# Splitting GpSimd's low-part subtraction of the input projection units into four instructions of 256 columns

## The chip, the cores and the metric

The kernel runs on one core of a Trainium2 chip. The metric is the device time of one execution, in microseconds (us). Each time is the median of several executions; the time before is 1633.45 us (three runs, 1633.38 to 1634.8).

## What is computed

One inference step of a two-layer streaming encoder, for 512 prompt tokens and 32 sample tokens (544 columns), model width 1024. Each layer, cut to what matters:

```
hn = rmsnorm(x, norm_mix)
parts = split_columns(hn @ w_in)          # w_in: 1024 x 2856, all four head groups
o_a = gated_delta(conv(q, k, v), ...)     # causal conv width 4, then chunk-wise delta rule
o_b = sink_attention(rope(s_q), ...)      # sliding window
o_c = mla_attention(...)                  # latent attention
o_d = c_b * causal_dwconv(c_c * c_x)
x = x + concat([o_a, o_b, o_c, o_d]) @ w_out
x = x + square(relu(rmsnorm(x) @ mlp_w1)) @ mlp_w2
x = x + (pl @ ple_w_proj) * sigmoid(rmsnorm(x) @ ple_w_gate)
```

## The kernel before

Activations lie with features on the 128 partitions and tokens along the columns. Weights come in *units* of 128 x 1024 (one output tile of 128 features against all 1024 input features, 512 KB). Every matmul by weights is done in three passes, for precision: each weight is split into a high part in a reduced format (`w_high`) and the rest (`w_rest`), each activation likewise, and the product adds high x high, high x rest and rest x high. A unit therefore passes four steps:

1. SyncE starts the DMA into one of two `raw` buffers (`load_unit`), once the unit that used the buffer has its low part made (`lo_done`).
2. ScalarE writes the high part (`high`, line 869) and raises `hi_done`. It first waits for the product of the unit two before, whose place in `w_high` it takes.
3. GpSimd writes the low part, raw minus high (`rest`, line 763), and raises `lo_done`.
4. TensorE multiplies (`product`, line 1702; `first_units`, line 1722, for the first two units of a layer; `unit_part`, line 1757, in quarters between attention tasks), after waiting for `lo_done`.

Units 0 to 22 of a layer are the input projection, 23 to 30 (`U_OUT`) the output projection, then come the MLP and the gate. All orders are written out by hand: every engine runs its own program in order, and semaphores tie them.

Around the change, in each layer: the first two units are multiplied tile by tile as VectorE makes the low part of `hidden` (line 1214) and, in the first layer, sums the squares (lines 1589 and 1590). Units 1 to 6 are q, k and v of the delta rule. For each, VectorE multiplies the product by the rms (line 1231), runs a convolution of four instructions (line 1247, then line 1250 three times, each waiting for the one before) and copies two tails of three columns (lines 1297 and 1298), after which ScalarE applies silu (line 1078). L2 norms of q and k follow (ScalarE lines 949 to 960, VectorE line 1571), and the first `prep` step on TensorE (line 1803) waits for all four. Units 7 to 14 are multiplied in halves with steps of the delta rule between them. Units 15 to 22 are spread over the attention: for each task TensorE makes scores, VectorE takes the minimum (line 1441), ScalarE the exponential, VectorE scales the probabilities (lines 1449 and 1450), TensorE turns them (line 1893) and multiplies by the values (line 1913). `rest` of unit u+2 is made when the product of unit u is done.

Of the kernel before, what the change touches and what calls it, by code (L numbers as in the profile page):

```python
# [18 lines left out]
F32 = mybir.dt.float32  # L19
F32R = mybir.dt.float32r  # L20
ALU = mybir.AluOpType
# [5 lines left out]
D = 1024  # L27
# [27 lines left out]
U_OUT = N_IN  # L55
# [59 lines left out]
def weight_no(u):  # L115

    return output_of(u) if u < U_PLE else O_PLE + u - U_PLE

def place_of(u):  # L120

    if u < U_MLP:
        return 2 * (u % 2)
    if u < U_PLE:
        g, i = divmod(u - U_MLP, 2 * KT)
        return (2 + 2 * KT * g + 7 * PAIRS * g + 2 * i) % RING
    return 2 * ((u - U_PLE) % 2)
# [61 lines left out]
def raw_place(l, u):  # L189

    a = 1 - l
    if u < U_MLP:
        return (u + l) % 2
    if u < U_PLE:
        return (a, 2, 3, 1 - a)[(u - U_MLP) % 4]
    return (a, 1 - a)[(u - U_PLE) % 2]
# [132 lines left out]
def build(nc, w_units, w_kv, params, consts, x_t, p_t, conv_state, ckv_cache, kpe_cache, k_cache, v_cache,  # L329
          s_state, sconv_state, y_t, gdn_s_p, gdn_s_s, conv_p, conv_s, swa_k_p, swa_k_s, swa_v_p, swa_v_s,  # L330
          ckv_p, ckv_s, kpe_p, kpe_s, sconv_p, sconv_s):
    with ExitStack() as ctx:
# [120 lines left out]
        def signal(name, per, head=0):  # L453
            every.append(Signal(ctx.enter_context(nc.semaphore(name)), per, head))
            return every[-1]
# [13 lines left out]
        lo_done = signal("lo_done", O_PLE + 2 + KT, 4)  # L469
# [118 lines left out]
        def in_ring(base, more, s, n):  # L588

            return (base if s < 4 else more[s // 2 - 2])[:, (s if s < 4 else s % 2) * 512:][:, 0:n * 512]  # L590

        def whi_at(l, s, n):
            return in_ring(whi, [w[l] if isinstance(w, list) else w for w in whi_more], s, n)

        def wlo_at(l, s, n):
            return in_ring(wlo, wlo_more, s, n)
# [4 lines left out]
        def raw_at(l, u):  # L601
            s = raw_place(l, u)
            return raw[:, s, :] if s < 2 else raw_more[:, s - 2, :]
# [39 lines left out]
        def mark(ins, sig):  # L643

            ins.then_inc(sig.sem, 1)
            sig.made += 1
# [103 lines left out]
        def _(pool):  # L750
# [8 lines left out]
            def rest(l, u):  # L759

                pool.wait_ge(*hi_done.at(l, weight_no(u) + 1))
                s = place_of(u)
                mark(pool.tensor_tensor(wlo_at(l, s, 2), raw_at(l, u), whi_at(l, s, 2).bitcast(F32), ALU.subtract), lo_done)  # L763

            def pair_rest(l, g, p, k):

# [10 lines left out]
            def rest_of(l, work):  # L777

                for w in work:
                    if len(w) == 1:  # L780
                        rest(l, *w)
                    else:
                        pair_rest(l, *w)
# [39 lines left out]
            for l in range(DEPTH):  # L823

                wait_apart(pool, normed.at(l, 0))
                mark(pool.memset(qkv[:, :, TOK:TOKP], 0.0), pad_done)
                for u in range(SPLIT):
                    rest(l, u)
                add_square(l, 0, KT - 1)
                for u in range(N_PRE):  # L830
                    mid_unit(l, 2 * u)
                    rest(l, u + SPLIT)
                    mid_unit(l, 2 * u + 1)
                for u in range(N_PRE, N_IN):
                    rest(l, u + SPLIT)
                for m in range(KT):
                    rest(l, U_OUT + SPLIT + m)
                    add_square(l, 1, m)
                for i in (2, 3):
                    rest(l, U_MLP + i)  # L840
                rest_of(l, due(0, -2, 2))
                for g in range(GROUPS):
                    rest_of(l, due(g, 0, 2 * KT))
                    for p in range(PAIRS):
                        rest_of(l, due(g, 2 * KT + 7 * p, 7))
                        if g == GROUPS - 1:
                            add_square(l, 2, 2 * p)
                            add_square(l, 2, 2 * p + 1)
                for m, u in enumerate(range(U_PLE + SPLIT, UNITS)):
                    rest(l, u)  # L850
                    if m:
                        add_square(l, 3, m - 1)
# [1358 lines left out]
```

## Time and profile before

| | |
|---|---|
| median of 3 runs | 1633.45 us (1633.38 to 1634.8) |
| the profiled execution | 1635.42 us, of which the span from first to last instruction 1633.6 us |
| TensorE busy | 1533.8 us (94%) |
| VectorE busy | 1042.8 us (64%) |
| GpSimd busy | 834.8 us (51%), 473 instructions |
| GpSimd line 763 | 146 instructions of 1024 columns, 46 of them for input projection units |
| granted TensorE clock | 0.981 on average |

PE is TensorE's matmul, PEld its weight load, DVE VectorE, ACT ScalarE, POOL GpSimd. Times in rows are in us from the start of the span, unless marked ns. An engine's busy time includes time in which a started instruction is held up, so a row that is longer than its like is an instruction that waited inside.

### The profile page before, as it was taken

Reading aid. Unit: us, or ns where it says so; the run is one execution under the profiler, and the core shown is the slowest. Engines: PE = TensorE matmul, PEld = TensorE weight load, DVE = VectorE, ACT = ScalarE, POOL = GpSimd, SP = SyncE. Lnnn points to the kernel's source line nnn. Section 1 sums busy time; section 2 is a strip of 40 time slices with the busy share of each in tenths; the row PEclk is TensorE's granted clock in tenths of the full one; section 3 lists DMA queues with packets and bytes.
Section 4 is the critical chain, followed back from the end, with each engine's and each line's share of the span. In section 5 each row is a group of like instructions: output and inputs, shape, how many; then the busy total and the mean of one; then the engine's idle time right before and its main releaser. Section 6 shows DMA issues by size and latency. Waiting matters only on the chain.

```text
span 1633.6 us, 33883 instructions
## 1 busy us (share of the span) xinstructions
PE 1533.8 (94%) x14198; PEld 1445.6 (88%) x14198; DVE 1042.8 (64%) x1754; ACT 669.9 (41%) x1186; POOL 834.8 (51%) x473
## 2 busy tenths in 40 slices
PE   6999998899999999998899999988999999999895
PEld 6889786699999999988898997767999999999795
DVE  6865567456848566595577645754478594756953
ACT  6521233444544343453345213334354444434432
POOL 3344121065766849486533531202668576684952
PEclk9999999899999999999999999998999999999998
DMA  5211011133241414213222110102332324141121
GB/s 196 77 41 41 27 40 40 33 118 104 69 139 52 130 53 123 77 48 106 83 79 65 41 41 27 40 27 60 116 92 89 104 75 134 52 130 52 54 90 68
DMA packets 43960, 123.81 MB, mean 76 GB/s; under 512 B 10976, under 2 KB 13792, under 8 KB 43552
## 3 DMA queue, kind: packets, MB, share of 16 engines
q1 hardware_dynamic: 43664, 119.86, 23.8%
q8 instruction: 113, 1.85, 0.5%
q10 hardware_dynamic: 144, 1.78, 0.3%
q14 instruction: 39, 0.32, 0.1%
HBM read 117.86 MB, written 3.76 MB: 74 GB/s over the span
## 4 chain that ended last, share of the span: by engine, by line
PE 74%; DVE 13%; POOL 6%; ACT 4%; issue 3%; DMA 0%; POOLq 0%; DVEq 0%; SPq 0%; ACTq 0%
PE psum_p L1702 39%; PE psum_t L1743 15%; PE psum_p L1757 6%; PE psum_t L1772 5%; POOL w_rest L775 3%; DVE conv_out L1250 2%; PE psum_p L1913 1%; POOL x_squares_summed L794 1%; PE psum_p L1722 1%; PE psum_p L1893 1%; DVE probs L1450 1%; PE psum_p L1765 1%; POOL w_rest L763 1%; PE psum_t L1883 1%; PE psum_t L1886 1%
## 5 line engine op out<-in xcount | busy, mean ns | idle before, releaser
L1702 PE MATMUL psum_p<-hidden,w_high 128*128 128x272 f32 x3904 | 661.8, 292 | 13.8 <-POOL w_rest L763 6.2
L1702 PEld LDWEIGHTS psum_p<-hidden,w_high 128*128 128x128 f32 x3904 | 557.8, 190 | 19.7 <-POOL w_rest L763 7.2
L763 POOL TENSOR_TENSOR w_rest<-raw,w_high 128x1024 fp32r<-128x1024 f32 x114 | 278.3, 2445 | 469.5 <-ACT w_high L869 469.5
L1702 PE MATMUL psum_p<-hidden,w_rest 128*128 128x272 f32 x1952 | 405.5, 289 | 0.0
L1702 PEld LDWEIGHTS psum_p<-hidden,w_rest 128*128 128x128 f32 x1952 | 308.1, 190 | 0.0
L775 POOL TENSOR_TENSOR w_rest<-w_sums,w_high 128x512 fp32r<-128x512 f32 x128 | 206.0, 1634 | 93.3 <-DVE w_sums L1493 55.3
L869 ACT ACTIVATE w_high<-raw 128x1024 fp32r<-128x1024 f32 x114 | 120.2, 1056 | 239.7 <-PE psum_p L1702 168.1
L1743 PE MATMUL psum_t<-hidden_split_a,w_high 128*128 128x272 f32 x896 | 178.6, 290 | 13.1 <-issue 7.7
L1743 PE MATMUL psum_t<-hidden_split_b,w_high 128*128 128x272 f32 x896 | 177.0, 288 | 0.4 <-DVE hidden_split_b L1509 0.4
L1743 PEld LDWEIGHTS psum_t<-hidden_split_a,w_high 128*128 128x128 f32 x896 | 140.0, 188 | 17.6 <-issue 16.1
L1743 PEld LDWEIGHTS psum_t<-hidden_split_b,w_high 128*128 128x128 f32 x896 | 140.3, 188 | 0.8 <-DVE hidden_split_b L1509 0.8
L1743 PE MATMUL psum_t<-hidden_split_b,w_rest 128*128 128x272 f32 x448 | 129.0, 288 | 0.0
L1743 PE MATMUL psum_t<-hidden_split_a,w_rest 128*128 128x272 f32 x448 | 128.8, 288 | 0.0
L883 ACT ACTIVATE w_high<-w_sums 128x512 fp32r<-128x512 f32 x128 | 79.7, 628 | 117.0 <-DVE w_sums L1491 61.5
L1517 DVE SCALAR_TENSOR_TENSOR rope_in<-psum_p,rms 128x544 f32<-128x544 f32 x64 | 46.2, 722 | 114.7 <-PE psum_p L1702 102.7
L763 POOL TENSOR_TENSOR w_rest<-raw_more,w_high 128x1024 fp32r<-128x1024 f32 x32 | 80.4, 2522 | 54.0 <-ACT w_high L869 54.0
L794 POOL TENSOR_TENSOR x_squares_summed<-x_squares_summed,x_squared 128x544 f32<-128x544 f32 x43 | 69.8, 1623 | 57.7 <-ACT x_squared L938 49.8
L1214 DVE SCALAR_TENSOR_TENSOR hidden<-x,parameters,hidden 128x544 fp32r<-128x544 f32 x48 | 77.5, 1615 | 30.4 <-ACT hidden L932 29.7
L908 ACT ACTIVATE hidden_parts<-rope_in 128x544 f32<-128x544 f32 x64 | 42.2, 659 | 128.4 <-DVE rope_in L1517 128.4
L1757 PE MATMUL psum_p<-hidden,w_high 128*128 128x272 f32 x512 | 91.7, 301 | 0.0
L775 POOL TENSOR_TENSOR w_rest<-raw,w_high 128x512 fp32r<-128x512 f32 x48 | 76.0, 1590 | 29.0 <-ACT w_high L883 29.0
L1743 PEld LDWEIGHTS psum_t<-hidden_split_a,w_rest 128*128 128x128 f32 x448 | 84.3, 188 | 0.0
(284 smaller groups left out, 2534.8 us busy)
## 6 DMA issues: line engine op xcount, KB each, us to landing
raw<-w_units SPq DMA_DIRECT2D x146, 512.0 KB, 3.6
raw_more<-w_units SPq DMA_DIRECT2D x64, 512.0 KB, 3.6
x<-x_t SPq DMA_DIRECT2D x8, 272.0 KB, 6.0
y_t<-y SPq DMA_DIRECT2D x8, 272.0 KB, 2.1
constants<-consts ACTq DMA_DIRECT2D x1, 1737.5 KB, 7.8
ple_in<-p_t SPq DMA_DIRECT2D x2, 544.0 KB, 4.5
constants<-consts SPq DMA_DIRECT2D x1, 1088.0 KB, 5.8
w_kv<-w_kv SPq DMA_DIRECT2D x2, 256.0 KB, 5.2
```

The source lines that it names most:

```text
L763: mark(pool.tensor_tensor(wlo_at(l, s, 2), raw_at(l, u), whi_at(l, s, 2).bitcast(F32), ALU.subtract), lo_done)
L775: mark(pool.tensor_tensor(wlo_at(l, s, 1), src, whi_at(l, s, 1).bitcast(F32), ALU.subtract), lo_done)
L794: ins = pool.tensor_tensor(sumx[:], sumx[:], sqx[:, m % 2, :], ALU.add)
L869: mark(act.activation(whi_at(l, place_of(u), 2), raw_at(l, u), ACT.Copy), hi_done)
L883: mark(act.activation(whi_at(l, s, 1), src, ACT.Copy), hi_done)
L908: link(act, act.activation(dst, two(xr[:]), ACT.Square), h_sq, l)
L1214: mark(dve.scalar_tensor_tensor(ha[l][:, m, 1, :], x[:, m, :], g, f(ha[l][:, m, 0, :]), ALU.mult, ALU.subtract), normed)
L1517: link(dve, dve.scalar_tensor_tensor(two(xr[:]), psum_of(l, o), 0.0, two(rms[:]), ALU.max, ALU.mult), freed, l)
L1702: ins = pe.matmul(pp[:, 2 * b + h, 0:HALF], w(l, s, 2)[:, cols(k)], rhs[:, k, part, h * HALF:(h + 1) * HALF], start=(n == 0 and z == 0), s ...
L1743: ins = pe.matmul(bank, w(l, s, 1)[:, j * P:(j + 1) * P], hs(l, j)[:, half, part, :], start=(j == 0 and z == 0), stop=(j == PAIRS - 1 and ...
L1757: ins = pe.matmul(pp[:, h, 0:HALF], w(l, s, 2)[:, k * P:(k + 1) * P], ha[l][:, k, half, h * HALF:(h + 1) * HALF], start=(k == 0 and z == 0 ...
L1772: ins = pe.matmul(dst[r, j * C:(j + 1) * C], lhsT(r), rhs(r), start=True, stop=True)
```

## The change

For units below `U_OUT`, `rest` issues four subtractions of 256 columns in place of one of 1024. The operands, the place in the order and both semaphores stay: the wait on `hi_done` stands before the first of the four, and `lo_done` is raised by the last. Other units keep the one instruction.

```diff
             def rest(l, u):
 
                 pool.wait_ge(*hi_done.at(l, weight_no(u) + 1))
-                s = place_of(u)
-                mark(pool.tensor_tensor(wlo_at(l, s, 2), raw_at(l, u), whi_at(l, s, 2).bitcast(F32), ALU.subtract), lo_done)
+                s, n = place_of(u), D // 4 if u < U_OUT else D
+                for a in range(0, D, n):
+                    ins = pool.tensor_tensor(wlo_at(l, s, 2)[:, a:a + n], raw_at(l, u)[:, a:a + n],
+                                             whi_at(l, s, 2).bitcast(F32)[:, a:a + n], ALU.subtract)
+                mark(ins, lo_done)
```

The order of GpSimd's instructions at the start of the first layer, before (`x_squares_summed` is the sum of squares, `hi_done` the signal of the high part):

```order
L763 TENSOR_TENSOR w_rest<-raw,w_high 128x1024 [waits hi_done] x2
L794 TENSOR_TENSOR x_squares_summed<-x_squares_summed,x_squared 128x544 [waits summed,squared]
L763 TENSOR_TENSOR w_rest<-raw,w_high 128x1024 [waits hi_done] x8
L805 TENSOR_TENSOR inverse_t<-lower_t_100,constants 128x384 [waits prep_u]
L807 TENSOR_TENSOR inverse_t<-constants,inverse_t 128x384 [waits masked]
```

and the same place in the changed kernel, as far as the second unit after the sum of squares (lines below the change have numbers higher by three):

```order
L764 TENSOR_TENSOR w_rest<-raw,w_high 128x256 [waits hi_done]
L764 TENSOR_TENSOR w_rest<-raw,w_high 128x256 x3
L764 TENSOR_TENSOR w_rest<-raw,w_high 128x256 [waits hi_done]
L764 TENSOR_TENSOR w_rest<-raw,w_high 128x256 x3
L797 TENSOR_TENSOR x_squares_summed<-x_squares_summed,x_squared 128x544 [waits summed,squared]
L764 TENSOR_TENSOR w_rest<-raw,w_high 128x256 [waits hi_done]
L764 TENSOR_TENSOR w_rest<-raw,w_high 128x256 x3
```

No instruction changed its place; in each unit three instructions without a wait stand behind the one that waits.

## Rows read from the trace of the kernel before

**Rows 1.** The page: busy shares, and the chain that ended last by engine

```profile
PE 1533.8 (94%) x14198; PEld 1445.6 (88%) x14198; DVE 1042.8 (64%) x1754; ACT 669.9 (41%) x1186; POOL 834.8 (51%) x473
PE 74%; DVE 13%; POOL 6%; ACT 4%; issue 3%; DMA 0%; POOLq 0%; DVEq 0%; SPq 0%; ACTq 0%
```

**Rows 2.** TensorE's waits, 183 to 320 us: total, times, longest

```profile
PE psum_p L1893 <- DVE probs L1450: 5.4, 5, 2.6
```

**Rows 3.** Instructions of a line: duration ns min/median/max, first and last start

```profile
L763 POOL TENSOR_TENSOR w_rest<-raw,w_high x114: 2339/2396/2946, 6.4 to 1607.4; 128x1024 fp32r<-128x1024 f32 x114
L775 POOL TENSOR_TENSOR w_rest<-w_sums,w_high x128: 1277/1741/1797, 404.2 to 1540.0; 128x512 fp32r<-128x512 f32 x128
L812 POOL TENSOR_TENSOR factor_t<-lower_t,constants x30: 992/1013/1495, 114.3 to 964.8; 128x384 f32<-128x384 f32 x30
L1250 DVE SCALAR_TENSOR_TENSOR conv_out<-conv_in,parameters,conv_out x36: 786/790/2818, 30.8 to 872.0; 128x547 f32<-128x547 f32 x36
```

**Rows 4.** Timeline of GpSimd, first layer: start, us, instruction, [idle before]

```profile
44.37 2.45 POOL L763 TENSOR_TENSOR w_rest<-raw,w_high 128x1024 fp32r<-128x1024 f32 x1 [4.93 <-ACT w_high L869]
52.23 2.71 POOL L763 TENSOR_TENSOR w_rest<-raw,w_high 128x1024 fp32r<-128x1024 f32 x1 [5.41 <-ACT w_high L869]
67.65 2.94 POOL L763 TENSOR_TENSOR w_rest<-raw,w_high 128x1024 fp32r<-128x1024 f32 x1 [5.12 <-ACT w_high L869]
```

**Rows 5.** Chain that ended last, 0 to 112 us: start, us, what

```profile
44.60 2.81 DVE conv_out L1250
```

**Rows 6.** Timelines of GpSimd and VectorE near 707 us, in the MLP

```profile
706.26 1.74 POOL L775 TENSOR_TENSOR w_rest<-raw_more,w_high 128x512 fp32r<-128x512 f32 x1
707.95 3.44 POOL L775 TENSOR_TENSOR w_rest<-raw,w_high 128x512 fp32r<-128x512 f32 x2
...
707.35 1.19 DVE L1493 TENSOR_TENSOR w_sums<-w_sums,raw 128x512 f32<-128x512 f32 x1
708.58 1.66 DVE L1495 TENSOR_TENSOR w_sums<-raw,w_sums 128x512 f32<-128x512 f32 x1
```

**Rows 7.** Small VectorE instructions, by line as in Rows 3

```profile
L1597 DVE TENSOR_SCALAR neg_sink<-parameters x2: 105/648/1192, 22.6 to 821.9; 128x4 f32<-128x4 f32 x2
...
L1297 DVE COPY conv_tail<-conv_in x6: 168/169/170, 33.3 to 71.2; 128x3 f32<-128x3 f32 x6
```

**Rows 8.** Timeline of TensorE in the convolution stage, first layer

```profile
49.44 0.67 PE L1702 MATMUL psum_p<-hidden,w_high 128*128 128x272 f32 x4
...
72.98 0.88 PE L1803 MATMUL psum_t<-level_x,constants 128*128 128x384 f32 x2 [1.63 <-DVE qkv L1571]
```

**Rows 9.** Timelines in the attention: TensorE's waits for probabilities, and GpSimd

```profile
208.46 0.52 PE L1893 MATMUL psum_p<-constants,probs 128*64 128x128 f32 x3 [0.41 <-DVE probs L1450]
222.49 0.52 PE L1893 MATMUL psum_p<-constants,probs 128*64 128x128 f32 x3 [0.23 <-DVE probs L1450]
257.53 0.33 PE L1893 MATMUL psum_p<-constants,probs 128*128 128x128 f32 x1 [0.75 <-DVE probs L1450]
280.83 0.55 PE L1893 MATMUL psum_p<-constants,probs 128*128 128x128 f32 x3 [1.43 <-DVE probs L1450]
...
278.22 2.34 POOL L763 TENSOR_TENSOR w_rest<-raw,w_high 128x1024 fp32r<-128x1024 f32 x1 [20.83 <-ACT w_high L869]
```

**Rows 10.** Both layers' starts: timelines of GpSimd, VectorE, TensorE, and the chain

```profile
6.42 2.35 POOL L763 TENSOR_TENSOR w_rest<-raw,w_high 128x1024 fp32r<-128x1024 f32 x1 [4.62 <-ACT w_high L869]
10.84 2.44 POOL L763 TENSOR_TENSOR w_rest<-raw,w_high 128x1024 fp32r<-128x1024 f32 x1 [2.07 <-ACT w_high L869]
...
13.91 10.82 PE psum_p L1722 x84
...
813.67 2.34 POOL w_rest L763
...
815.43 1.16 DVE L1214 SCALAR_TENSOR_TENSOR hidden<-x,parameters,hidden 128x544 fp32r<-128x544 f32 x1
...
831.64 0.57 PE L1702 MATMUL psum_p<-hidden,w_high 128*128 128x272 f32 x1 [2.34 <-POOL w_rest L763]
```

## The prediction

> **What bounds the kernel now.** I read the page first: TensorE is busy 94% of the span and 74% of the chain that ended last, VectorE 13%, GpSimd 6% [rows 1]. So the change can win or lose only where TensorE waits. The next view was therefore TensorE's waits by stage, then the timelines of GpSimd and VectorE around each changed instruction.
>
> Two things are to be seen. First, a VectorE instruction with two SBUF inputs that meets a running GpSimd subtraction is held until that ends: line 1250 takes 0.79 us alone and up to 2.82 us [rows 3]. At 44.60 one took 2.81 us; the GpSimd instruction from 44.37 ended at 46.82, so VectorE finished 0.59 us behind it [rows 4, 5]. It lost 2.0 us. Second, after a subtraction the held VectorE instruction goes next, even where GpSimd has another ready: near 707 us subtractions of 512 columns and VectorE's sums alternate, GpSimd starting every 1.70 us instead of 1.28 [rows 3, 6]. A turn of VectorE therefore costs GpSimd about 0.45 us, and by the same arithmetic 0.5 us for the slightly longer line 1250.
>
> **The cost of a quarter.** The trace before has no subtraction of 256 columns. Undisturbed, 1024 columns take 2.34 us and 512 take 1.28 [rows 3]: 2.08 ns a column and 0.21 us fixed. For 256 columns that gives 0.745 us; the line checks itself at 384 columns (1.01 worked out, 0.99 measured, other operands). Four make 2.98 us, 0.64 more than one. From below, the fixed part could overlap with the instruction before (2.34 in all); from above, a quarter cannot cost more than the 0.99 us of 384 columns (3.96 in all). I take 0.745, as the line fits three sizes. The 46 changed units cost GpSimd 29 us of its own time, nearly all of it under TensorE's products, since `lo_done` is needed only one whole product after the high part starts (48 matmuls, 6.2 us at the pace of rows 10).
>
> **The losses** are where TensorE waits for the low part itself.
> - Start of layer 2: the subtraction from 813.67 ends the wait for the first product [rows 10]. It gets 0.64 longer, and line 1214 from 815.43, which today is held by it, now gets its turn in the middle (0.4): +1.05.
> - Third unit of layer 2: TensorE waited 2.34 us for GpSimd at 831.64 [rows 10], no VectorE instruction in the way: +0.6.
> - Start of layer 1: the subtractions from 6.42 and 10.84 [rows 10] run beside line 1214 and the sums of squares. With alternation the first ends at about 10.45 instead of 8.77, the second at 15.2 instead of 13.28. TensorE begins 1 us late, but it used to stall until 13.91 for a held line 1214, which now ends at 12.2. It then needs the second unit at 15.2; 78 of 96 matmuls are left, at 10.82/84 us each [rows 10] 10.05 us, so it ends at 25.25 instead of 24.73. With some of the slow first matmuls moved later: +0.6 (0 to 1.5).
> Together +2.25.
>
> **The gain in the convolutions.** In the view of the chain this stage looks like VectorE's, but TensorE is busy from 43 to 71 us and idles only 1.63 us, at 72.98 [rows 8]. That caps the gain at about 1.6 us a layer. I walk the three held convolutions of Rows 4. Held by quarters, each of the three instructions of line 1250 loses 0.4 us instead of one losing 2.0. But then quarters are left over, and what comes next is the pair of three-column copies. Whether so small a copy is held decides the sum. Line 1297 has never met GpSimd (168 to 170 ns); its nearest relative, the four-column line 1597, has: 105 ns once and 1192 ns once [rows 7]. I take it that they are held, each by a quarter.
> - Unit at 44.37: three instructions save 0.8, a copy loses 0.55; the next evacuation then waits for TensorE's product, done about 49.35 [rows 8]: 0.25 ahead.
> - Unit at 52.23: one convolution instruction (0.43) and two copies (0.6 each) are held instead of 2.0 us: 0.7 ahead. The ScalarE chain and line 1571 carry that on, about even.
> - Unit at 67.65: one convolution instruction, two copies and line 1571 are held, 2.2 us against 2.0: 0.55 ahead at the end.
> So 0.55 us a layer. If the copies pass freely, the same walk gives 1.5 at the second unit, 2.4 at the third, cut by the cap to 1.6.
>
> By the Trainium skill (VectorE: DVE Perf Modes, Mode 2×_2P) a one-source copy inside SBUF takes the mode that uses both read ports when the outermost dimension is even, or odd and equal on both sides, which three columns to three columns are. By that rule the copies are held and the sum is the one I forecast; no row here shows it for three columns.
>
> **The gain in the attention.** Changed units are made here up to the one at 255 us; the instruction at 278.22 belongs to the output projection and stays whole, as does the next [rows 9]. TensorE's waits for probabilities sum to 5.4 us [rows 2], of which 1.43 at 280.83 and the longest, 2.6, thus stay. Left are 0.41, 0.23 and 0.75 [rows 9]. With quarters the scaling is held 0.4 to 0.6 us instead of 2, so the first two go. The third gives nothing: behind it VectorE has four more instructions that quarters hold, one each (about 0.5), and TensorE next waits for what follows them. So 0.64 a layer (0.3 to 1.4).
>
> **The sum.** Losses 2.25, gains 2 x (0.55 + 0.64) = 2.4: net -0.1 us. The profiled execution (1635.42, span 1633.6) was 2 us over the median; its differences carry over unchanged. So 1633.45 - 0.1 = 1633.3. Within 0.2% (3.3 us) is what a measurement of this kernel can't tell from no change.
>
> **Rivals.**
> 1. *The copies are not held* (25%). Line 1297's constant 169 ns doesn't speak against it. Gains 2 x (1.6 + 0.64) = 4.5, net -2.2: 1631.2.
> 2. *Slower: the four keep the port* (10%). Three of the four have no wait, and GpSimd may never give VectorE its turn between them. Then each held instruction loses 0.6 more than today: in each layer three convolutions and the two of line 1571 (2.2), three scalings (1.8); at the starts 1.2 in layer 1 (two subtractions that hold line 1214) and 1.2 in layer 2. 2 x 4.0 + 2.4 = 10.4: 1643.9. For it: in Rows 6 every subtraction has a wait, if one long satisfied. Against: the next one's record there starts 0.05 us before the last ends, so it was ready too, and VectorE still went first. It decides as soon as VectorE is passed over at two of three boundaries. 
> 3. *A quarter costs its upper bound*, 0.99 us (10%). Then the losses grow by 0.9 at each of four subtractions that TensorE waits for, and held instructions wait 0.25 longer, which takes the convolution gain: +3.6 + 1.1: about 1638.
> 4. *More comes free* (5%): VectorE's shorter holds also take the third attention wait and part of TensorE's waits for ScalarE: 1629.5.
> The forecast itself has 50%, its own range 1632 to 1635.
>
> **Chances.** Faster by over 0.2%: rival 4 and a tail of rival 1, 0.08. Slower by over 0.2%: rivals 2 and 3 but for a part of 3, 0.17. Same: 0.75. The range must reach rival 1 and its tail, and nearly rival 3: 1630 to 1638.
>
> **What would show it.** In the profile after: quarters of 0.74 us, 1.2 to 1.25 where VectorE takes turns; line 1250 at most 1.25 us, three in a row in a held convolution; lines 1297 and 1298 (three higher after) at 0.6 to 0.75 us at their longest; TensorE's wait before line 1803 (after: 1806) near 1.1 us instead of 1.63; the first product of layer 2 a microsecond later against the end of the layer before it; scaling at 206 and 220 us below 1 us and the waits of 0.41 and 0.23 gone, those of 1.43 and 2.6 there. Wrong would make me: line 1250 at 3 us or more (rival 2), copies at 0.17 us throughout (rival 1), quarters near 1 us undisturbed (rival 3).

## The result and the profile after

The changed kernel takes 1636.22 us in the median of 20 executions (1633.43 to 1640.49), the kernel before 1633.22 in 20. The ratio is 1.0022 with a 95% interval of 1.0014 to 1.0031: 3.6 us slower (2.3 to 5.1), where I had forecast 0.1 us less. 1636.22 lies inside the range of 1630 to 1638, but "no change" was wrong. The two profiled executions differ by 0.5 us only (1635.95 and 1635.42, spans 1634.1 and 1633.6), because executions of one kernel differ by 7 to 9 us. So the profiles are compared below stage by stage, and over many kernels. Of the 12 executions of e13_late_26 below, one took 5110 us and is left out of the median.

The page of the kernel after (busy shares, and the chain by engine), to be read beside [rows 1]:

```profile
PE 1537.4 (94%) x14198; PEld 1448.7 (89%) x14198; DVE 1030.0 (63%) x1754; ACT 669.9 (41%) x1186; POOL 872.5 (53%) x611
PE 76%; DVE 11%; POOL 6%; ACT 4%; issue 3%; DMA 0%; SPq 0%; POOLq 0%; DVEq 0%; ACTq 0%
```

GpSimd has 138 instructions and 38 us more, VectorE is busy 13 us less: its held instructions are shorter. TensorE is busy 3.6 us *more* with the same 14198 matmuls. That is the first sign: the work didn't grow, so some of it ran slower.

A second sign is the mean granted clock, which is on record for each execution. It is 0.9799 on average in the 20 executions after, and 0.9840 in the 110 executions of the kernel before that were measured beside the experiments. Among those 110 it goes with the time: the median is 1635.6 us in the 23 at 0.982 or less, 1633.5 in the 36 at 0.983 or 0.984, 1631.5 in the 51 above. (The records of the clock begin only at 11 to 19 us, see e12_all_filled, so the start of layer 1 isn't in these means.)

What happened to the instructions of a line (columns as in [rows 3]), and TensorE's waits from 20 to 183 us and from 183 to 320 us (as [rows 2]):

```profile
L764 POOL TENSOR_TENSOR w_rest<-raw,w_high x252: 718/745/2901, 6.4 to 1607.9; 128x256 fp32r<-128x256 f32 x92, 128x1024 fp32r<-128x1024 f32 x34
L1253 DVE SCALAR_TENSOR_TENSOR conv_out<-conv_in,parameters,conv_out x36: 787/1144/1231, 32.1 to 874.8; 128x547 f32<-128x547 f32 x36
L1300 DVE COPY conv_tail<-conv_in x12: 170/584/595, 35.3 to 876.0; 128x3 f32<-128x3 f32 x12
L1301 DVE COPY conv_tail<-conv_in x12: 153/155/161, 35.4 to 876.5; 128x3 f32<-128x3 f32 x12
...
PE psum_t L1806 <- DVE qkv L1574: 0.7, 1, 0.7
...
PE psum_p L1896 <- ACT probs_t L1011: 6.4, 6, 2.0
PE psum_p L1896 <- DVE probs L1453: 4.0, 2, 2.6
```

The group of line 764 mixes 184 quarters with 68 subtractions of 1024 columns; a quarter alone has a median of 732 ns. Four that nothing disturbs start every 0.68 us and are done in 2.77 to 2.81 us (22 units), as here at 74.59:

```profile
74.59 2.80 POOL L764 TENSOR_TENSOR w_rest<-raw,w_high 128x256 fp32r<-128x256 f32 x4 [3.23 <-ACT w_high L872]
```

The convolution's instruction is held to at most 1.23 us instead of 2.82, and TensorE's wait behind the convolutions is 0.69 us instead of 1.63 [rows 8]. In the attention the waits of 0.41, 0.23 and 0.75 us for VectorE [rows 9] are gone, but the longest wait for ScalarE has become 2.0 us, where it was 1.7.

The start of layer 2 holds the surprise. Timelines of GpSimd and TensorE, then the granted clock by stretches (columns: length, TensorE busy and its matmuls, granted clock, DMA share, GB/s):

```profile
813.88 7.48 POOL L764 TENSOR_TENSOR w_rest<-raw,w_high 128x256 fp32r<-128x256 f32 x8
817.21 0.88 PE L1725 MATMUL psum_p<-hidden,w_high 128*128 128x272 f32 x4 [2.38 <-POOL w_rest L764]
834.65 1.20 PE L1705 MATMUL psum_p<-hidden,w_high 128*128 128x272 f32 x4 [2.69 <-POOL w_rest L764]
...
814.00:816.00 2.00, 0.82 (x7) 1.00 0.06 18
816.00:818.00 2.00, 0.79 (x5) 0.92 0.00 0
818.00:820.00 2.00, 2.00 (x11) 0.50 0.83 215
820.00:822.00 2.00, 2.00 (x14) 0.72 0.37 60
822.00:824.00 2.00, 2.00 (x19) 1.00 0.74 191
```

TensorE waits 2.38 us here; before it was 1.50:

```profile
816.06 0.77 PE L1722 MATMUL psum_p<-hidden,w_high 128*128 128x272 f32 x4 [1.50 <-POOL w_rest L763]
```

Behind the longer wait the granted clock falls to 0.5, 1.2 GHz instead of 2.4, and TensorE does 11 matmuls in two microseconds instead of 18. From its last matmul of layer 1 (817.21 - 2.38 = 814.83) to the third unit's product (834.65) it needs 19.82 us. Before it was 831.64 [rows 10] less 816.06 - 1.50, or 17.08. Of the 2.74 us, 0.88 is the first wait, 0.35 the third unit's (2.69 against 2.34), and 1.5 the slow matmuls.

The same is seen in the attention. TensorE of the kernel after, and its clock:

```profile
254.19 0.34 PE L1871 MATMUL psum_t<-qkv,state 64*64 64x64 f32 x4 [0.47 <-ACT chain_v L986]
260.43 0.30 PE L1896 MATMUL psum_p<-constants,probs 128*128 128x128 f32 x1 [2.03 <-ACT probs_t L1011]
268.22 0.41 PE L1896 MATMUL psum_p<-constants,probs 128*128 128x128 f32 x2 [0.80 <-ACT probs_t L1011]
...
258.00:261.00 3.00, 0.97 (x11) 1.00 0.56 175
261.00:264.00 3.00, 3.00 (x16) 0.55 0.00 0
```

and of the kernel before, where the clock stays at 1.00 through this stretch:

```profile
255.19 0.34 PE L1868 MATMUL psum_t<-qkv,state 64*64 64x64 f32 x4 [0.47 <-ACT chain_v L983]
261.48 0.30 PE L1893 MATMUL psum_p<-constants,probs 128*128 128x128 f32 x1 [1.11 <-ACT probs_t L1008]
267.76 0.41 PE L1893 MATMUL psum_p<-constants,probs 128*128 128x128 f32 x2 [0.80 <-ACT probs_t L1008]
```

Up to 255 us the change is 1.0 us ahead (254.19 against 255.19). Then the wait of 0.75 us has not vanished but moved behind the scores and joined the one of 1.11: the row that ends it stands 6.24 us behind L1871 after and 6.29 behind L1868 before. The clock falls behind the joined wait, and at the 0.80 us wait the change is 0.46 us behind.

**Two measures that can be read in any profile.** M1, start of layer 2: from TensorE's last matmul of layer 1 to the third unit's product. M2, attention: from the row L1871 to the one with [0.80 <-ACT probs_t], in layer 1 and in layer 2. The profiles of all kernels give (each from the difference of two such rows, whose line numbers differ a little from kernel to kernel; e1 to e15 are described below):

| kernel | first wait of layer 2 | M1 | wait or waits in M2 | M2, layers 1 and 2 |
|---|---|---|---|---|
| before | 1.50 | 17.08 | 0.75 + 1.11 | 12.57, 14.03 |
| after | 2.38 | 19.82 | 2.03 | 14.03, 15.49 |
| e1_starts | 2.40 | 19.85 | 0.75 + 1.12 | 12.57, 14.03 |
| e2_convs | 1.50 | 17.08 | 0.75 + 0.45 | 13.41, 13.35 |
| e3_attention | 1.49 | 17.06 | 2.03 | 15.40, 12.52 |
| e4_no_starts | 1.49 | 17.07 | 2.03 | 14.02, 15.48 |
| e5_fill_start | 0.55 behind the fill | 18.47 | 2.03 | 15.50, 15.53 |
| e6_fill_third | 1.49 | 17.07 | 0.76 + 1.11 | 12.59, 12.57 |
| e7_without_22 | 1.50 | 17.08 | 0.76 + 0.45 or 1.11 | 13.34, 12.59 |
| e8_first_only | 2.40 | 19.51 | 0.76 + 1.11 | 12.58, 12.58 |
| e9_both | 1.48 | 17.05 | 0.75 + 1.11 | 14.04, 12.58 |
| e10_whole_fill | 1.50 | 17.08 | 0.76 + 1.12 | 12.58, 14.04 |
| e11_both_warm | 1.49 | 17.07 | 0.75 + 1.12 | 12.57, 12.63 |
| e12_all_filled | 0.59 behind the fill | 18.53 | 0.76 + 1.11 or 0.45 | 12.58, 13.41 |
| e13_late_26 | 2.34 | 19.45 | 0.75 + 1.11 | 12.57, 12.58 |
| e14_late_13 | 1.93 | 19.03 | 0.75 + 1.11 or 0.45 | 14.06, 13.41 |
| e15_both_with_22 | 1.50 | 17.07 | 2.03 | 15.43, 13.98 |

M1 hardly scatters: 17.05 to 17.08 in ten profiles with the first unit whole and on time. M2 does: 12.5 to 12.6 us if the clock holds, 13.3 to 14.1 or 15.4 to 15.5 if it falls once or twice. With the joined wait of 2.03 it was above 12.65 in 9 of 10 layers (mean 14.74), with the waits apart in 10 of 24 (mean 13.05).

Two things belong to this. First, a second wait of 0.45 instead of 1.11 means that the clock fell behind the first one, of 0.75, and that the scores between them ran slower and filled part of the second (e2_convs: the wait ends at 256.54, and from 258 to 260 us the clock is 0.50). That was so in 5 of the 24 layers. So the length of one wait doesn't decide alone. Second, the falls might only have moved to another place of the attention. On average that doesn't show: from 250 to 325 and from 1050 to 1135 us together, the clock was at half for 34 us on average in the five profiles with the joined wait, and for 27 us in the other twelve.

### The profile page after: what moved, and what is told of

It is laid out like the page before. It is cut to its first block, busy times and chain, and to the rows that moved or that the text cites. A ratio compares the mean times of both kernels' runs of the same rounds, so it can differ in the third digit from the quotient of the medians.

```text
span 1634.1 us, 34021 instructions
## 1 busy us (share of the span) xinstructions
PE 1537.4 (94%) x14198; PEld 1448.7 (89%) x14198; DVE 1030.0 (63%) x1754; ACT 669.9 (41%) x1186; POOL 872.5 (53%) x611
## 4 chain that ended last, share of the span: by engine, by line
PE 76%; DVE 11%; POOL 6%; ACT 4%; issue 3%; DMA 0%; SPq 0%; POOLq 0%; DVEq 0%; ACTq 0%
PE psum_p L1705 40%; PE psum_t L1746 15%; PE psum_p L1760 6%; PE psum_t L1775 5%; POOL w_rest L778 3%; PE psum_p L1725 2%; PE psum_p L1916 1%; PE psum_p L1896 1%; POOL x_squares_summed L797 1%; POOL w_rest L764 1%; PE psum_t L1886 1%; PE psum_t L1889 1%; PE psum_p L1768 1%; DVE conv_out L1253 1%; DVE mla_q L1284 1%
## 5 line engine op out<-in xcount | busy, mean ns | idle before, releaser
L764 POOL TENSOR_TENSOR w_rest<-raw,w_high 128x256 fp32r<-128x256 f32 (+1 forms) x252 | 316.2, 1279 | 443.1 <-ACT w_high L872 424.2
L778 POOL TENSOR_TENSOR w_rest<-w_sums,w_high 128x512 fp32r<-128x512 f32 x128 | 206.0, 1633 | 93.3 <-DVE w_sums L1496 55.3
```

The lines of the kernel that those rows point to most:

```text
L764: ins = pool.tensor_tensor(wlo_at(l, s, 2)[:, a:a + n], raw_at(l, u)[:, a:a + n], whi_at(l, s, 2).bitcast(F32)[:, a:a + n], ALU.subtract)
L778: mark(pool.tensor_tensor(wlo_at(l, s, 1), src, whi_at(l, s, 1).bitcast(F32), ALU.subtract), lo_done)
```

## Experiments

Each kernel is the one after with the edit shown. The first set puts quarters on some of the units only. The time is the median against that of the kernel before in the same runs; behind it stands the ratio, which need not agree with the difference of medians (in e4_no_starts they are 1.8 us apart). Where both are given, the interval is that of the ratio.

| kernel | median | before | ratio (95% interval) |
|---|---|---|---|
| e1_starts | 1637.04 | 1633.03 | 1.0028 (1.0016 to 1.0039) |
| e2_convs | 1630.53 | 1633.03 | 0.9981 (0.9972 to 0.9991) |
| e3_attention | 1632.83 | 1633.03 | 1.0001 (0.9992 to 1.0010) |
| e4_no_starts | 1631.41 | 1633.03 | 1.0001 (0.9992 to 1.0010) |
| e5_fill_start | 1633.61 | 1632.58 | 1.0000 (0.9991 to 1.0010) |
| e6_fill_third | 1629.28 | 1632.58 | 0.9976 (0.9965 to 0.9987) |
| e7_without_22 | 1630.72 | 1632.58 | 0.9989 (0.9980 to 0.9998) |
| e8_first_only | 1635.57 | 1632.58 | 1.0017 (1.0007 to 1.0028) |
| e9_both | 1625.26 | 1633.60 | 0.9955 (0.9938 to 0.9971) |
| e10_whole_fill | 1631.02 | 1633.60 | 0.9987 (0.9976 to 0.9997) |
| e11_both_warm | 1625.08 | 1633.60 | 0.9950 (0.9934 to 0.9967) |
| e12_all_filled | 1629.73 | 1633.60 | 0.9977 (0.9968 to 0.9987) |
| e13_late_26 | 1636.73 | 1632.54 | 1.0022 (1.0010 to 1.0034) |
| e14_late_13 | 1636.68 | 1632.54 | 1.0026 (1.0011 to 1.0040) |
| e15_both_with_22 | 1630.54 | 1632.54 | 0.9986 (0.9974 to 0.9998) |

### e1_starts

```diff
-                s, n = place_of(u), D // 4 if u < U_OUT else D
+                s, n = place_of(u), D // 4 if u < 3 else D
```

> Only the first three input projection units of each layer are subtracted in quarters, the others whole. Theory 1, the clock: the late last quarters at the two starts cost more than their own time, because TensorE runs its next products slowly behind them. At the start of layer 1 the first product after the wait near 15.3 us is slow (about 0.22 us a matmul instead of 0.125), and the step behind it at 27.1 us in the kernel before comes 2.0 to 2.5 us late; at the start of layer 2 TensorE idles about 2.4 us instead of 1.5 and the granted clock then falls to 0.5, so that this product takes 13 us instead of 11.6. Nothing gives it back: +3 to +4.5 us in the median. Theory 2, my sum: the waits cost their own time, 0.6 + 1.05 + 0.6, no more: +2.25 us. Theory 3, the loss lies in the units behind: within 1 us of before.

Measured: +4.0 us. TensorE's waits at the start of layer 2 in its profile are those of the kernel after, and so is M1 (19.85):

```profile
816.17 0.97 PE L1725 MATMUL psum_p<-hidden,w_high 128*128 128x272 f32 x4 [2.40 <-POOL w_rest L764]
833.62 1.27 PE L1705 MATMUL psum_p<-hidden,w_high 128*128 128x272 f32 x4 [2.70 <-POOL w_rest L764]
```

Three units of each layer carry the whole loss. My sum (2.25) lies outside the interval of 2.6 to 6.4 us, and theory 1 inside. One thing of theory 1 didn't show: at the start of layer 1 TensorE was at full pace behind its wait at 15.31 us, and the first evacuation stood at 27.76, only 0.64 us behind the 27.12 of before.

### e2_convs

```diff
-                s, n = place_of(u), D // 4 if u < U_OUT else D
+                s, n = place_of(u), D // 4 if 3 <= u < 9 else D
```

> Only units 3 to 8 of each layer (those made beside the convolutions of the second and third stage of the input projections) are subtracted in quarters. All theories that keep my reading of the convolutions: TensorE's wait at 73 us falls from 1.63 to about 0.7, and the time falls by 0.9 us a layer where nothing else changes: -1 to -2 us. If the loss of the whole change lies here after all (theory 3): 0 to +1.5 us.

Measured: -2.5 us (by the ratio -3.1, from -4.6 to -1.5). The gain of the convolutions is real, and with 0.9 us a layer larger than my 0.55.

### e3_attention

```diff
-                s, n = place_of(u), D // 4 if u < U_OUT else D
+                s, n = place_of(u), D // 4 if 9 <= u < U_OUT else D
```

> Only units 9 and above, up to the last input projection unit, are subtracted in quarters; some ten of them are made beside the first third of the attention. Theory 1, the clock: the waits of 0.41 and 0.23 us are gone and those of 0.75 and 1.11 us fall together into one of about 2.0; the granted clock then falls to half for 3 us in this stretch (as it does in the changed kernel after 260 us), which gives the microsecond back and more: -0.5 to +1.5 us. Theory 2, waits alone: the microsecond a layer stays won: -1.3 to -2 us. In the profile: granted clock in the 20 us behind 260 us below 0.9 (theory 1) or 1.00 (theory 2).

Measured: -0.2 us (by the ratio +0.2, -1.3 to +1.6), where waits alone make it -1.3 or better. The clock of layer 1 behind the joined wait fell twice in a row (M2 15.40), in layer 2 not at all (12.52). Layer 1:

```profile
261.00:264.00 3.00, 3.00 (x12) 0.50 0.00 0
264.00:267.00 3.00, 3.00 (x20) 0.58 0.00 0
```

### e4_no_starts

```diff
-                s, n = place_of(u), D // 4 if u < U_OUT else D
+                s, n = place_of(u), D // 4 if 3 <= u < U_OUT else D
```

> All the input projection units but the first three of each layer are subtracted in quarters. Theory 1: the loss of the starts (3 to 4.5 us) is gone, the gain of the convolutions stays, and the attention is about even: -0.5 to -2 us against before. Theory 2 (waits alone; both gains stay): -2.5 to -4 us. Theory 3, the loss lies behind the starts: +1 to +3 us.

Measured: -1.6 us in the median, +0.2 by the ratio (-1.3 to +1.6). The loss of the starts is gone and theory 3 with it. But this kernel isn't faster than e2_convs, which has fewer quarters: the attention's quarters bring nothing in sum, though each profile has them 0.9 us a layer ahead at 255 us.

### e5_fill_start

```diff
+            def fill(n):
+                for _ in range(n):
+                    pe.matmul(pt[:, 3, 0:HALF], ones, cst[:, 0:HALF], start=True, stop=True)
+
...
                     b, s = slot(l, u), place_of(u)
+                    if i == 0 and l:
+                        fill(4)
                     if k == 0:
```

> The changed kernel, and ahead of the wait for the first low part of layer 2 TensorE runs four matmuls of constants into a bank that nobody reads (2.2 us at the duration of the sum of squares, 0.54 us each). The wait for GpSimd stays as long as it was; only TensorE isn't idle in it. Clock theory: the granted clock stays at 1.00 near 817 us, the product behind the wait runs at full pace, and of the 2.4 us that this start lost in two profiles with quarters there 1.3 to 1.6 come back: about 1634.5 to 1635, +1.5 us against before. Rival, the wait itself costs (or the quarters' reads slow TensorE down): nothing comes back, 1636.2 to 1637, and the product behind it is as slow as before or the fall is still there.

Measured: +1.0 us (by the ratio 0.0, -1.5 to +1.6), against +3.6 (2.3 to 5.1) without the fill: the intervals are apart. TensorE and its clock at the start of layer 2 (each matmul of `fill` stands in the rows as two, so the four are x8):

```profile
814.35 2.00 PE L1712 MATMUL psum_t<-constants 128*128 128x272 f32 x8
816.89 0.77 PE L1731 MATMUL psum_p<-hidden,w_high 128*128 128x272 f32 x4 [0.55 <-POOL w_rest L764]
...
816.00:818.00 2.00, 1.45 (x10) 1.00 0.12 25
818.00:820.00 2.00, 2.00 (x18) 1.00 0.95 236
```

The first product starts 2.54 us behind the last matmul of layer 1, about as late as after (2.38), but the clock holds and it runs at 18 matmuls in two microseconds. M1 is 18.47 instead of 19.82. Adding four useless matmuls made the kernel faster. (A surprise beside it: the third unit's wait is still 2.69 us, and the clock didn't fall behind it in this profile.)

### e6_fill_third

```diff
-                s, n = place_of(u), D // 4 if u < U_OUT else D
+                s, n = place_of(u), D // 4 if 3 <= u < 9 else D
...
                             pe.wait_ge(*c_r.at(l, 1))
+                    if u == 2:
+                        fill(4)
                     product(l, u, u, ha[l], range(KT), between=lambda: mid_unit(l, 2 * u))
```

> Quarters for units 3 to 8 only (e2_convs: 1630.5 us), and in both layers the same four matmuls of constants stand ahead of the third unit's product, where TensorE is idle for 2.34 us in every profile, whatever is changed, and the clock falls in layer 2 in every one. Clock theory: no fall near 831 us (and none near 29 us), 1.5 us back in layer 2 and up to 1.5 in layer 1: 1627.5 to 1629.2 us. Rival: an idle stretch of this length isn't what makes it fall, or the fall costs nothing: 1630 to 1631 us.

Measured: -3.3 us (ratio -3.9), 0.8 us better than e2_convs both ways of reckoning. In its profile the clock is 1.00 where it was 0.50 in the kernel before:

```profile
826.91 2.00 PE L1712 MATMUL psum_t<-constants 128*128 128x272 f32 x8
829.42 0.74 PE L1705 MATMUL psum_p<-hidden,w_high 128*128 128x272 f32 x4 [0.51 <-POOL w_rest L764]
...
829.00:832.00 3.00, 2.58 (x20) 1.00 0.50 153
832.00:835.00 3.00, 3.00 (x26) 1.00 0.27 59
```

```profile
832.00:835.00 3.00, 3.00 (x15) 0.50 0.55 175
```

(the second block is the kernel before). What I expected of "every profile" was too much: in those of e5_fill_start and e7_without_22 the clock held behind this wait without a fill, so the fill wins its 1.5 us only in the executions in which it would have fallen. In the eleven profiles with no fill there, it fell behind this wait in nine.

### e7_without_22

```diff
-                s, n = place_of(u), D // 4 if u < U_OUT else D
+                s, n = place_of(u), D // 4 if 9 <= u < 22 else D
```

> As e3_attention (units 9 and above in quarters, 1632.8 us), but unit 22, the last of the input projections, whole again. Clock theory: the waits of 0.75 and 1.11 us stay apart instead of becoming one of 2.03, the clock falls no more often there than in the kernel before, and the gain of 0.86 us a layer stays: 1631.2 to 1632 us. Rival, the gain is given back by something else in the attention: 1632.5 to 1633.3 us. Should unit 22 carry the gain itself, which my prediction denies, the offset at 255 us shows it (0 instead of -0.86).

Measured: -1.9 us (ratio -1.8, -3.3 to -0.3). Leaving one unit of 14 whole makes 1.7 us of difference to e3_attention in the median, in the direction of the clock theory. In its profile the waits are 0.76, and in layer 2 1.11 behind it; nowhere is there one of 2.03. Alone the pair isn't enough, since the intervals overlap; e15_both_with_22 is the second pair. The mean granted clock of all executions points the same way: 0.9823 in e3_attention, 0.9837 here.

### e8_first_only

```diff
-                s, n = place_of(u), D // 4 if u < U_OUT else D
+                s, n = place_of(u), D // 4 if u == 0 else D
```

> Only the first unit of each layer in quarters. Clock theory: at the start of layer 2 TensorE idles 2.4 us, the clock falls, and the first evacuation of the layer comes 2.4 us later against the end of the layer before it; the start of layer 1 costs 0 to 0.6 us, the third unit nothing: +2.2 to +3 us, 1635.2 to 1636. My sum (1.05 at layer 2, at most 0.3 at layer 1, no clock): +1.1 to +1.4 us. If the second and third unit carried the loss of e1_starts (+4.0): below +1 us.

Measured: +3.0 us (ratio 2.8, 1.1 to 4.6). One subtraction a layer costs what my whole list of losses was to cost. M1 is 19.51: the 2.4 us of the clock theory over 17.08, and the third unit's 0.35 isn't there. My sum for it was 1.1 to 1.4, at the edge of the interval.

### e9_both

```diff
-                s, n = place_of(u), D // 4 if u < U_OUT else D
+                s, n = place_of(u), D // 4 if 3 <= u < 22 else D
...
+                    if u == 2:
+                        fill(4)
```

> The two edits that gained, together: quarters for units 3 to 21 (first three and unit 22 whole), and the four matmuls of constants ahead of the third unit's product. If the gains are separate, -3.3 (e6_fill_third) and -1.9 us (e7_without_22): -4.5 to -5.5 us against before, about 1627.5 us. If they feed on the same falls of the clock: -3.5 us.

Measured: 1625.26 us, -8.3 in the median and -7.3 by the ratio (-10.1 to -4.7). It is with e11_both_warm the fastest kernel of the study, faster than both kernels compared. I had expected -4.5 to -5.5, if the gains were separate. The gains add up, and perhaps more than that; e10_whole_fill shows one reason.

### e10_whole_fill

```diff
-                s, n = place_of(u), D // 4 if u < U_OUT else D
+                s, n = place_of(u), D
...
+                    if u == 2:
+                        fill(4)
```

> All units whole as before, with the four matmuls of constants ahead of the third unit's product alone. Clock theory: the fall near 831 us and that near 29 us are gone where they came: -0.8 to -2 us. Rival, the 1.2 us that e6_fill_third won over e2_convs are scatter: within 0.5 us of before.

Measured: -2.6 us (ratio -2.1, -3.9 to -0.5). Four useless matmuls a layer are a gain on their own. But the gain is smaller here than beside quarters. In layer 2, from the third unit's product to TensorE's wait for the convolutions, this profile is 0.78 us shorter than the kernel before (830.03 to 874.26 against 831.64 to 876.65); e6_fill_third is 1.43 us shorter than e2_convs (829.42 to 872.03 against 830.59 to 874.63). With whole units TensorE waits part of the time won away again, for VectorE: 1.80 us instead of 1.64 at 874.26, and 0.30 at 843.96, where it didn't wait before.

### e11_both_warm

As e9_both, and:

```diff
+            def warm(n):
+                w = whi_at(0, place_of(0), 2)
+                pe.wait_ge(*hi_done.at(0, 1))
+                for _ in range(n):
+                    pe.matmul(pt[:, 3, 0:HALF], w[:, 0:P], w[:, 0:HALF], start=True, stop=True)
...
+                if l == 0:
+                    warm(12)
```

> As e9_both, and at the start of layer 1, from the moment at which the first high part is there (about 6.3 us), TensorE runs twelve matmuls of that part into a bank that nobody reads, before the first product at 9.5 us. In every profile the first matmuls of layer 1 take 0.226 us instead of 0.125, until 14 us in most and until 19 us in some, with and without quarters, though the profile's rows give the clock as 1.00 there. If this is TensorE's clock, not yet granted because it has been idle, the slow stretch ends earlier against the first product: the first evacuation (27.1 us before) comes 0.3 to 1 us earlier and never 2.2 us later, -0.5 to -1.5 us against e9_both. If the slow matmuls are waits for data (loads of hidden or weights): no change, or later by what the twelve delay.

Measured: 1625.08 us, even with e9_both, so the expected gain of 0.5 us is a miss. TensorE of this kernel:

```profile
6.36 3.09 PE L1718 MATMUL psum_t<-w_high 128*128 128x272 f32 x12 [6.36 <-ACT w_high L872]
10.98 0.74 PE L1737 MATMUL psum_p<-hidden,w_high 128*128 128x272 f32 x4
...
14.01 0.77 PE L1737 MATMUL psum_p<-hidden,w_high 128*128 128x272 f32 x4 [1.21 <-POOL w_rest L764]
```

The mechanism is there: four matmuls take 0.74 us from 10.98 on, where the kernel after needs 1.11 at 12.78 (next fence). So the slow pace is not a wait for data: it ends earlier, with the same data, if TensorE has worked earlier. But the pace of these matmuls wasn't on the path. TensorE only waits longer for the second low part, until 14.01.

### e12_all_filled

As e11_both_warm, and:

```diff
-                s, n = place_of(u), D // 4 if 3 <= u < 22 else D
+                s, n = place_of(u), D // 4 if u < 22 else D
...
+                    if i == 0 and l:
+                        fill(4)
```

> As e11_both_warm, but the first three units of each layer in quarters too, with matmuls of constants also ahead of the first product of layer 2. Here the starts cost only their waits, without the clock: by the profiles 0.64 (start of layer 1), 0.9 and 0.35 (layer 2): +1.9 us against e11_both_warm. If quarters at the starts cost something else than the waits and the clock, it stays at the +4 us of e1_starts.

Measured: -3.9 us, 4.6 more than e11_both_warm where I expected 1.9. The fills at layer 2 worked (M1 18.53; 17.07 + 0.9 + 0.35 makes 18.3). Another 2.24 us came at the start of layer 1, where the third unit's product begins at 30.09 instead of 27.85:

```profile
15.25 1.04 PE L1739 MATMUL psum_p<-hidden,w_high 128*128 128x272 f32 x4 [1.82 <-POOL w_rest L764]
...
14.00:16.00 2.00, 0.75 (x4) 0.89 1.14 306
16.00:18.00 2.00, 2.00 (x11) 0.50 1.03 404
18.00:20.00 2.00, 2.00 (x14) 0.76 0.96 406
```

TensorE, warm early and through early, now idles 1.82 us until the second low part, which the quarters have made late, and the clock falls. In the kernel after the same matmuls are just as slow, but with 1.00 in the row of the clock:

```profile
12.78 1.11 PE L1725 MATMUL psum_p<-hidden,w_high 128*128 128x272 f32 x4
15.26 1.28 PE L1725 MATMUL psum_p<-hidden,w_high 128*128 128x272 f32 x4 [0.92 <-POOL w_rest L764]
17.70 0.66 PE L1725 MATMUL psum_p<-hidden,w_rest 128*128 128x272 f32 x2
...
16.00:18.00 2.00, 2.00 (x11) 1.00 1.12 401
```

That 1.00 is not a measurement. The first record of the clock in this trace begins at 18.98 us, and a stretch without a record is shown as 1.00. The first matmul at the short interval of 0.125 us starts at 19.03. In all 17 profiles it is so: the first record begins between 11.14 us (e11_both_warm) and 19.13 (e5_fill_start), matmuls start every 0.226 us ahead of it and every 0.125 behind it. 0.226 us is also the pace at a granted clock of 0.50, 1.2 GHz. So TensorE very likely starts the program at 1.2 GHz, though no record says so.

### e13_late_26 and e14_late_13

```diff
-                s, n = place_of(u), D // 4 if u < U_OUT else D
+                s, n = place_of(u), D
...
+        pause, _ = place("pause", [P, 32])
...
                 mark(pool.memset(qkv[:, :, TOK:TOKP], 0.0), pad_done)
+                for i in range(26 if l else 0):
+                    pool.memset(pause[:, i:i + 1], 0.0)
```

with 13 instead of 26 in e14_late_13.

> All units whole, as in the kernel before; only at the start of layer 2 GpSimd clears 26 single columns (about 0.035 us each) ahead of the subtraction of the first low part, which makes it 0.9 us late without any quarter. Clock theory, by the length of the idle stretch alone: TensorE idles 2.4 us instead of 1.5, the clock falls near 817 us, the product behind it takes 13 us instead of 11.6, and the first evacuation of layer 2 comes 2.4 us later against the end of layer 1; +2.2 to +2.6 us in the median. Rival, it is the quarters (VectorE's turns between them, more traffic of GpSimd's) that make this start slow: +0.9 us, clock at 1.00.

> The same with 13 columns: 0.45 us late, TensorE idle for 1.95 us. If the fall depends on the length of the idle stretch alone and 1.5 us has never brought it here while 2.03 us nearly always has: the clock falls in the profile or not, +0.5 us without it and +2 us with it; a median between the two means that it falls in some executions. Rival (only quarters bring it): +0.45 us and no fall.

Measured: +4.2 us (ratio 3.6, 1.6 to 5.6) and +4.1 us (ratio 4.2, 1.8 to 6.5). e13_late_26 at the start of layer 2, and then e14_late_13:

```profile
813.42 0.92 POOL L832 MEMSET pause<- 128x1 f32 x26
816.70 1.00 PE L1728 MATMUL psum_p<-hidden,w_high 128*128 128x272 f32 x4 [2.34 <-POOL w_rest L765]
...
818.00:820.00 2.00, 2.00 (x11) 0.50 0.86 265
```

```profile
817.49 0.77 PE L1728 MATMUL psum_p<-hidden,w_high 128*128 128x272 f32 x4 [1.93 <-POOL w_rest L765]
...
820.00:822.00 2.00, 2.00 (x11) 0.50 0.68 119
```

No quarter, and the same fall, in e13_late_26 with about the lateness of the kernel after. It is the idle stretch of TensorE and not the quarters that brings it, and 1.93 us of it was enough (M1 19.03: 0.43 of wait and 1.5 of clock), where 1.50 us never did it in ten profiles. The results lie 1.2 to 2.3 us over what M1 says (2.4 and 1.9); the first is still within the interval, the second at its lower end. The clock can account for the rest: its mean over the executions is 0.0019 and 0.0027 below that of the kernel before, and one fall of 3.4 us to half in 1634 is 0.0010. By that estimate there were 1.9 and 2.6 more falls and not one, which at 1.5 us each, with 0.9 and 0.43 us of wait, makes 3.7 and 4.3 us. Why a late start of layer 2 brings falls elsewhere stays open.

### e15_both_with_22

As e9_both, with:

```diff
-                s, n = place_of(u), D // 4 if 3 <= u < 22 else D
+                s, n = place_of(u), D // 4 if 3 <= u < U_OUT else D
```

> As e9_both (1625.3 us), but unit 22 in quarters as well. Clock theory for the attention: the waits of 0.75 and 1.11 us become one of 2.03 again, and what e7_without_22 won over e3_attention (2 us) is lost: 1627 to 1628.5 us. Rival, the difference between those two was scatter and unit 22 costs nothing: 1625 to 1626 us.

Measured: 1630.54 us, -2.0 (ratio -2.3, -4.2 to -0.3), against -8.3 (-7.3, -10.1 to -4.7) of e9_both: the intervals are apart, by 0.5 us. It lost more than the 1.7 to 3.2 us expected. The mean granted clock is 0.9823 against 0.9847, by the estimate above 2.2 falls more. The 2.03 us wait is back in both layers:

```profile
260.01 0.39 PE L1900 MATMUL psum_p<-constants,probs 128*128 128x128 f32 x1 [2.03 <-ACT probs_t L1011]
1063.98 0.30 PE L1900 MATMUL psum_p<-constants,probs 128*128 128x128 f32 x1 [2.03 <-ACT probs_t L1011]
```

Unit 22 in quarters costs 1.7 to 6.3 us by the medians of the two pairs, 2.0 and 5.0 by the ratios. M2 says 1.7 us a layer (14.74 against 13.05), 3.4 in all.

## Why the prediction was wrong

**Mechanism: right. Price of four quarters: too high.** One quarter takes 732 ns in the median, where 745 was worked out (the 745 in the row above is the median of a mixed group and agrees by luck). But four in a row overlap a little: 2.77 to 2.81 us instead of 2.98, so a unit gets 0.45 longer and not 0.64. The lower bound, an overlap of the fixed part, was partly true. The turns went as Rows 6 had shown: four quarters with turns took 4.30 us from 45.13 in the kernel after, and no convolution instruction took over 1.23 us. Rivals 2 and 3 are out.

**The copies: half right.** Line 1300 is held (584 ns in the median), line 1301, which follows at once, never is (at most 161). By the Trainium skill (VectorE: DVE Perf Modes, Mode 2×_2P) both should use both ports; the trace agrees for the first. The second started 0.02 us ahead of GpSimd's next quarter (55.56 and 55.58) or met no further one, and neither was held. Why is open. Rival 1 was thus half true.

**The convolutions' gain: too small.** 0.94 us less wait a layer (1.63 to 0.69) instead of 0.55: one copy was held behind a convolution, where I had two in two of the three units.

**The attention's gain up to 255 us: 0.87 us** (1.00 less 0.13 that the change was ahead at 184 us) instead of 0.64.

**"The third gives nothing": the step that failed most.** The prediction put the third attention wait at no gain and no loss. As a sum of waits it is right, 0.75 came back as part of the next one. But I took waits as additive: 0.75 + 1.11 apart and 2.03 in one piece cost the same idle time and not the same clock. By M2 this is 3.4 us over two layers, and e15_both_with_22 against e9_both shows the sign (the intervals are apart).

**The loss at the start of layer 2: mis-sized.** Predicted 1.05 + 0.6. The waits gave 0.88 + 0.35, less than predicted, since four quarters cost 0.45 more and not 0.64. The fall of the clock behind the first gave 1.5 more, in each profile with the first low part 0.4 us or more late and no fill, in none of ten with it on time. The trace before had told it: the clock stood at 0.50 from 832 to 835 us, behind the wait of 2.34 us [rows 10], and I priced idle time only: the slower matmuls behind a longer wait stood in the sum at nothing, without a reason.

**The loss at the start of layer 1: 0.64 us where the pace was the same, as predicted (0.6)**, but 2.25 in the profile after, as the first matmuls stayed at 0.226 us until 19 us. It is so in 2 of 3 profiles with quarters on all three units and in 3 of 12 of the others (the two kernels with twelve matmuls ahead of the first product not counted). Whether they make it likelier is open.

Put together with the measured terms: starts 2.74 + 0.64 or more, convolutions -1.9, attention -1.7, unit 22 +3.4, so +3.2 us and up, against 3.6 measured. The mean granted clock gives nearly the same: 0.0042 less is by the estimate above 4.0 falls, 6.0 us, less the 1.7 us by which the waits alone are shorter: 4.3. The forecast had no rival in which the clock answers to the length of an idle stretch; all my prices came from rows at full clock.

## What to carry to other kernels

A wait of TensorE is priced by two numbers: its length, and whether the clock falls behind it; a change that makes a wait of 1.5 us 0.4 us longer, or joins two short ones, can cost 1.5 us more than the sum. Length isn't all: here a wait of 0.75 us had a fall behind it in 5 of 24 layers. So look at the granted clock behind each wait before and after, and where a wait can't be avoided, try matmuls of constants in it (-2.6 us here for eight matmuls in 1633 us). And cut up only what somebody is held by: the first units of a layer, for which TensorE itself waits, are better whole.

## What the hardware showed that I hadn't expected

- Each fall at the start of layer 2 lasted 3.4 us and cost 1.5 us of TensorE's time; it came behind idle stretches of 1.93, 2.34, 2.38 and 2.40 us, and not behind 1.50. Behind one of 2.34 or 2.69 (third unit) it came in some profiles and not in others, so executions of one kernel differ in it. The mean granted clock of an execution goes with its time (1631.5 us at 0.985 and more, 1635.6 at 0.982 and less, in 110 of the kernel before), so that is much of their scatter.
- Matmuls of constants in a wait of TensorE's make the kernel faster: behind them the next product ran at 18 matmuls in two microseconds instead of 11.
- At the start of a program matmuls take 0.226 us instead of 0.125. The rows of the clock show 1.00 there, but only because its first record begins where the pace changes (18.98 and 19.03 us in the kernel after). Twelve matmuls from 6.36 us on end the slow pace at 10.98 us, where without them no matmul was at full pace before 13.9.
- Quarters without waits overlap: 0.73 us each, but one starts every 0.68, and four take 2.80.
